# Weight low parts of the second FFN: from GpSimd to the vector engine, each behind an eviction

## What is computed

```python
def swiglu(x, wg, wu, wd):
    return (jax.nn.silu(x @ wg) * (x @ wu)) @ wd
...
        h_p = h_p + swiglu(rmsnorm(h_p, norm_ffn_g[layer]), w_gate[layer], w_up[layer], w_down[layer])
        h_s = h_s + swiglu(rmsnorm(h_s, norm_ffn_g[layer]), w_gate[layer], w_up[layer], w_down[layer])
```

## Time and profile before

| | us |
|---|---|
| median of 3 runs | 2636.41 |
| lowest and highest of them | 2635.61, 2637.15 |
| the profiled execution | 2633.95 |
| its span | 2632.0 |
| TensorE busy in it | 2543.6 (97%) |
| vector engine busy | 1715.1 (65%) |
| ScalarE busy | 999.8 (38%) |
| GpSimd busy | 997.0 (38%) |

### The profile page before, as it was taken

How to read it: one execution, slowest core, us unless ns; L and a number is a source line. 1 busy time by engine, 2 the same in 40 slices (tenths; PEclk the granted TensorE clock), 3 DMA queues, 4 the chain that set the end, 5 groups by cost and what they waited for, 6 DMA issues and landing times.

```text
span 2632.0 us, 44346 instructions
## 1 busy us (share of the span) xinstructions
PE 2543.6 (97%) x17835; PEld 2430.5 (92%) x17835; DVE 1715.1 (65%) x1937; ACT 999.8 (38%) x1480; POOL 997.0 (38%) x616
## 2 busy tenths in 40 slices
PE   8999989999999999999999999999989999999997
PEld 7989988999999999988888888879889999999997
DVE  4244498456666766768787878895785555567555
ACT  4122153222222111267777777774432222221113
POOL 4643335888885876100000000000246555552110
PEclk9999999999999999999999999999999999999999
DMA  4111223544445665322222231244222222234211
GB/s 131 41 42 34 74 81 90 169 150 157 154 145 197 231 205 169 146 90 80 66 89 83 88 96 61 82 145 158 73 81 82 66 87 76 82 138 164 91 66 74
DMA packets 271134, 284.93 MB, mean 108 GB/s; under 512 B 14810, under 2 KB 213778, under 8 KB 270930
## 3 DMA queue, kind: packets, MB, share of 16 engines
q1 hardware_dynamic: 252770, 272.79, 31.5%
q10 hardware_dynamic: 18160, 9.31, 1.2%
HBM read 195.37 MB, written 86.67 MB: 107 GB/s over the span
## 4 chain that ended last, share of the span: by engine, by line
PE 80%; DVE 10%; issue 4%; ACT 2%; DMA 2%; POOL 1%; SPq 1%; ACTq 0%; DVEq 0%; POOLq 0%
PE ps L1318 24%; PE ps L1407 16%; PE ps L1146 10%; PE aux L1536 8%; PE aux L1318 4%; PE ps L1453 3%; PE ps L1481 3%; PE ps L1435 2%; PE ps L1801 2%; PE ps L1465 2%; PE aux L1547 1%; PE aux L1500 1%; DMA a_plain<-hid_kept 1%; PE aux L1489 1%; DVE sp_part_odd L2985 1%
## 5 line engine op out<-in xcount | busy, mean ns | idle before, releaser
L1065 POOL TENSOR_TENSOR ring<-w_raw,ring 128x512 fp32r<-128x512 f32 x44 | 61.7, 1401 | 844.0 <-ACT ring L1969 844.0
L1318 PE MATMUL ps<-s_hi,ring 128*128 128x264 f32 x2016 | 338.6, 286 | 9.9 <-DVE h L2744 6.5
L1318 PEld LDWEIGHTS ps<-s_hi,ring 128*128 128x128 f32 x2016 | 285.3, 190 | 11.4 <-DVE h L2744 7.2
L2933 DVE TENSOR_TENSOR h<-h,ps 128x1056 f32<-128x1056 f32 x144 | 180.4, 1253 | 149.3 <-PE ps L1407 147.8
L1065 POOL TENSOR_TENSOR ring<-ring_plain,ring 128x512 fp32r<-128x512 f32 x90 | 158.7, 1781 | 266.9 <-DVE w_hi_plain L2615 218.4
L1407 PE MATMUL ps<-s_hi 128*128 128x352 f32 x1008 | 219.7, 326 | 10.2 <-DVE h L2933 3.7
L1407 PE MATMUL ps<-s_lo,s_hi 128*128 128x352 f32 x1008 | 217.8, 324 | 0.0
L1407 PE MATMUL ps<-s_hi,s_lo 128*128 128x352 f32 x1008 | 217.7, 323 | 0.0
L1969 ACT CAST ring<-ring_plain 128x512 fp32r<-128x512 f32 x90 | 52.1, 619 | 411.7 <-DVE ring_plain L2608 405.3
L1318 PE MATMUL ps<-s_lo,ring 128*128 128x264 f32 x1008 | 205.8, 286 | 0.0
L2003 ACT CAST s_hi<-a_plain 128x2112 fp32r<-128x2112 f32 x22 | 43.3, 1968 | 386.5 <-PE ps L1407 309.2
(11 more groups left out here) (386 smaller groups left out, 6581.6 us busy)
## 6 DMA issues: line engine op xcount, KB each, us to landing
hid_kept<-h SPq DMA_DIRECT2D x44, 528.0 KB, 6.2
a_plain<-hid_kept SPq DMA_DIRECT2D x44, 528.0 KB, 5.6
w_raw<-in_w_gate_dram SPq DMA_DIRECT2D x44, 512.0 KB, 5.0
w_hi<-kept_hi SPq DMA_DIRECT2D x30, 512.0 KB, 4.0
w_lo<-kept_lo SPq DMA_DIRECT2D x30, 512.0 KB, 5.4
h_kept<-h SPq DMA_DIRECT2D x24, 528.0 KB, 3.1
h<-h_kept SPq DMA_DIRECT2D x24, 528.0 KB, 6.5
w_raw<-in_w_down_dram SPq DMA_DIRECT2D x24, 512.0 KB, 4.3
```

The source lines that it names most:

```text
L1065: gp.tensor_tensor(lo, src, as32(hi), ALU.subtract).then_inc(part_ready, 1)
L1318: last = mm(pairs[bank][:, c, 0:QC], w[:, ks], x[:, k, c * QC:c * QC + QC], start=(fresh and k == 0 and n == 0), stop=(k == HK - 1 and n = ...
L2933: vec.tensor_tensor(chunks(h[:, n, :]), chunks(h[:, n, :]), out, ALU.add).then_inc(tile_out, 1)
```

## The change

In layer 1 GpSimd stops after unit 2; from unit 3 on (the fourth) the vector engine makes the low parts, 7 for each of 19 units. Its loop over u makes those of unit u+1 at seven places between its evictions. Each waits for its high part, for the low part before it (also where that is its own), and for products 5 and 6 for the sum of `turn_4`.

```diff
@@ GpSimd, def ffn(layer)
                 for u, m in OPENING:
                     part_low(layer, u, m)
-                for u in range(2, NU):
+                for u in range(2, NU if layer == 0 else 3):
                     for m in UNIT_ORDER:
                         part_low(layer, u, m)
@@ vector engine, def ffn(layer, event, first_in)
+                def next_low(u, m):
+                    if layer == 0 or u + 1 >= NU:
+                        return
+                    b11, b21, b12, b22 = sources(layer, u + 1)
+                    hi, lo = ring_slot(layer, u + 1, m)
+                    src = {1: b11, 2: b21, 3: b22, 7: b12}.get(m)
+                    dve.wait_ge(part_hi, parted_at(layer, u + 1, m))
+                    dve.wait_ge(part_ready, parted_at(layer, u + 1, m) - 1)
+                    if m in (5, 6):
+                        dve.wait_ge(turned_done, turned_sum(layer, u + 1, 4))
+                    vec.tensor_tensor(lo, src if src is not None else ring_sum(layer, u + 1, m), as32(hi), ALU.subtract)\
+                        .then_inc(part_ready, 1)
+
                 for u in range(2, NU):
                     if u > 2:
                         t1_scaled(u)
+                    next_low(u, 1)
                     t6_added(u, b)
                     t3_added(u, b)
                     c22_added(u, c)
@@
                     if u + 1 < NU:
                         turn_4(layer, u + 1)
                         turn_3(layer, u + 1)
+                    next_low(u, 6)
+                    next_low(u, 5)
                     if u % 2:
                         act_rescaled(u // 2)
+                    next_low(u, 7)
                     c11_scaled(u, a)
+                    next_low(u, 4)
+                    next_low(u, 2)
                     if u + 1 == NU:
                         for f in range(2):
                             hid_low(layer, 0, f)
                     c12_added(u, c)
+                    next_low(u, 3)
                     if u % 2:
                         hidden(u // 2)
                     else:
```

## The result

| | before, us | changed, us |
|---|---|---|
| median of 6 runs of each | 2636.01 | 2644.48 |
| lowest and highest | 2630.89, 2637.38 | 2639.0, 2647.43 |
| the profiled execution | 2633.95 | 2639.0 |
| its span | 2632.0 | 2636.2 |

The ratio is 1.0035, with a 95% interval of 1.0021 to 1.0049: slower by 5.5 to 12.9 us, 9.2 in the middle. The forecast was 11.1 us more (a ratio of 1.0042), and 2647.5. The interval's lower end, 0.21%, lies only just above the 0.2% that the prediction called the least that can be told from no change.

What follows compares the result with a forecast made beforehand. TensorE was taken to bound the kernel, with no slack to regain losses. Odd units 7.2, unit 2 2.2 and a clock drop 1.7 summed to 11.1 us more, giving 2647.5 us; range 2639.0 to 2652.5 us.

Steps and rivals of the forecast that it cites:

- Nothing to gain from a freer GpSimd: Second FFN: TensorE never waits for GpSimd there, so work taken off GpSimd is worth nothing by itself.
- The slack of 0.19 us at c11_scaled: End of odd units: c11_scaled can come only 0.19 us later before TensorE waits, too little for three low parts.
- the sign: What would show it right: TensorE waiting for c11_scaled nine times, 0.6 to 0.8 us each, at ends of odd units.
- The cost of a low part, 0.60 us, and 0.79 behind a wait: Vector engine: a low part costs 0.60 us start to start, 0.79 where the next waits for its result.
- The rescaling at 1.80: Vector engine's 128x1584 rescaling: with GpSimd idle beside it, 1.80 us everywhere, in place of 2.90 in unit 13.
- Odd units, 7.2 us: Units 3, 5, ..., 19: TensorE starts 0.70 us late plus 0.11 for the restart, 0.8 us nine times.
- Unit 2, 2.2 us: End of unit 2: low parts 6, 5 and 7 move c11_scaled from 1957.72 to 1959.90, all of it TensorE's loss.
- The clock, 1.7 us: Behind unit 2's hole of some 2.8 us: one drop of TensorE's clock to 1.2 GHz; bounds 0 and 3.4 us.
- Even units, nothing: Even units: no loss, with 0.8 us of cover at c11_scaled and 1.4 us at t6_added.
- The rival that low part 1 blocks t6_added: Even units: high part 1 comes 2 us later, delaying t6_added; 0.6 us lost in nine units, 2652.5 us; chance 0.04.
- not slower: Odd units' stall does not come, c11_scaled ending 0.7 us earlier than reckoned; only unit 2's 1.5 us left, 2637.9; chance 0.10.
- the rescaling stays at 2.90: Odd units: the rescaling's length is not GpSimd's doing, each 1.1 us later, 9.9 us more, 2657.4 us; chance 0.06.

Runs made afterwards that it cites:

- experiment 2: Changed kernel with c11_scaled ahead of low parts 6, 5 and 7 in odd units; median 2636.56 us, ratio 1.0012 to the kernel before.
- experiment 7: Changed kernel with low part 7 made twice in odd units, the first followed by a wait; median 2651.65 us, ratio 1.007 to the kernel before.
- experiment 6: Changed kernel without each low part's wait for the one ahead, except at the takeover from GpSimd; median 2642.74 us, ratio 1.0037 to the kernel before.
- experiment 8: Changed kernel with GpSimd given 12 chained 128x128 multiplications beside the rescaling of odd units; median 2654.68 us, ratio 1.0087 to the kernel before.
- the second: Profile of the changed kernel timed again with no edit; median 2645.77 us, ratio 1.0049 to the kernel before.
- experiment 3: Changed kernel with GpSimd keeping unit 3 too, the vector engine beginning with unit 4; median 2641.25 us, ratio 1.0032 to the kernel before.
- experiment 4: Changed kernel with low parts on the vector engine from unit 4 only, in odd units behind c11_scaled; median 2636.37 us, ratio 1.0011 to the kernel before.
- experiment 5: Changed kernel with c11_scaled ahead of low parts 6, 5 and 7 in odd units and unit 2; median 2634.02 us, ratio 1.0005 to the kernel before.

## Why the prediction was right, point by point

- **Nothing to gain from a freer GpSimd.** Right. With GpSimd idle, TensorE's list of waits got longer and no shorter.
- **The slack of 0.19 us at c11_scaled.** Right, by experiments 2 and 7: take the low parts from in front of it and the loss of odd units is nil, put 0.72 us more there and 0.72 more is lost. The size of the waits was called 0.6 to 0.8 us, and they are 0.53: the sign took the lateness, 0.69, for the idle time that the trace lists.
- **The cost of a low part, 0.60 us, and 0.79 behind a wait.** Right for low parts 6 and 5: from 2181.71 to the rescaling at 2183.10 they take 1.39 us, which is 0.79 and 0.60. The rule of the Trainium skill (VectorE: DVE Perf Modes, "The DRAIN you can't avoid") would have taken 2.1 us off; experiment 6 took the waits away and the trace got 1.8 us shorter, so they do cost. The price is not the same behind every wait: in experiment 7 it was 0.72.
- **The rescaling at 1.80.** Right in the units that count, and it decided the size. At 2.90 each odd unit would have lost 1.1 us more. "Everywhere" was too much: in unit 21 it went from 1.80 to 3.50 us. The rival's remark that the turns take 0.68 us whether GpSimd works beside them or not rests on little, since only turn_3 has GpSimd beside it, in part; the low parts in experiment 8 show that instructions of this size can be stretched.
- **Odd units, 7.2 us.** The stretch from t3_added of unit 3 to that of unit 21 grew by 7.84 us. Term a little too small: a pair of units takes 41.82 us or so for 40.96, where 0.8 was reckoned. TensorE starts 0.69 us late, as reckoned; behind that the way to the next t3_added is 0.15 us longer, not 0.11, and the following even unit often loses 0.05.
- **Unit 2, 2.2 us.** Measured 2.21 (19.61 for 17.40).
- **The clock, 1.7 us.** Not in the first profile; in the second it fell, at a cost of 1.5 us. Over the five profiles with a hole of 2.8 us it fell in four, at 1.5 us in three and 2.7 in one (the two drops in a row of the prediction's bound, though not quite its 3.4); over the six with a shorter one (2.44 us in experiment 6, 1.47 and less in the others) never. As a likely term it was well placed. Whether it falls in a given run, nothing here tells beforehand.
- **Even units, nothing.** Right: no wait for L2744 in the changed kernel. But in unit 3 its cover does not hold once the queue is shifted: in experiments 3, 4 and 5 it is L2744 that TensorE waits for there. The rival that low part 1 blocks t6_added was real, though not in the place where I priced it. Its price was added up wrong, too: nine times 0.6 is 5.4 us, so 2652.9 and not 2652.5, which is outside the range and not at its end.
- **The sum.** 9.4 us without the clock and 11.1 with it; in the trace the stretch grew by 10.05 and, with the clock's fall, by 11.57. The medians say 9.2 and 12.9, with intervals (5.5 to 12.9 and 9.2 to 16.3) that hold both. So the medians bear out the size only roughly; it is the trace that bears out the terms. In the first profile two errors partly cancel: odd units were put 0.6 us too low, the clock 1.7 too high. Of the rivals, "not slower" fell with the nine waits, "the rescaling stays at 2.90" with 1801 ns.
- **The level.** 2647.5 was 3 us above the first median of 2644.48; the clock, where it does not fall, is 1.5 us of that. How often it fell in the six runs is not known, and medians of the kernel before differ by more than the rest (2636.01 here, 2631.62 to 2633.49 in the experiments).

## What to carry to other kernels

Where one engine is the bound, the share of free time of a helper says little; what counts is how much time lies between the end of a certain eviction and the moment at which the bound engine needs it. Read that slack in the timeline before moving work onto the evicting engine, and put the work behind the eviction with the least of it. Then follow what was pushed back: the next eviction in the queue, and the instruction that waits on another engine with others behind it, are where the loss turns up again.

## What was unexpected

- A hole of 2.8 us in TensorE's work was followed by a fall of its clock to 1.2 GHz in four of five profiles: three times for some 3.4 us at a cost of 1.5, once for 6.8 at a cost of 2.7. One of 2.44 us in one profile was not.
- Small GpSimd instructions of 128x128 elements stretch the vector engine's 128x512 ones: from 688 to 780 ns in the mean. In the kernel before turn_3 kept to 0.68 us, though a longer one of GpSimd's began 0.23 us after it.
- In the changed kernel the rescaling of unit 21 takes 3.50 us for 1.80: it comes later against GpSimd's next work and now lies wholly beside it.
- Handing the low parts from one engine to the other costs 1.0 us by itself when the taker has an eviction queued behind its first wait (experiment 3).
